# Down product of a sparse-expert layer on one core: three products of 224 columns into one PSUM place, three homes for the column parts, sums read straight from PSUM

## The reference

```python
def first_block(x, ...):
    ...                                   # gated mixing and dilated attention, w_out
    x = x + peer(rms_norm(x, norm2_g[layer]), w_query[layer], sub_keys[layer],
                 expert_u[layer], expert_v[layer])
    return rms_norm(x, final_norm_g)

def peer(xn, ...):                        # 8 heads pick 16 of 128 * 128 experts for each token
    ...
    act = jax.nn.gelu(jnp.einsum('td,thkd->thk', xb, u).astype(jnp.float32))
    return jnp.einsum('thk,thkd->td', (g * act).astype(xb.dtype), expert_v[e])

def second_block(x, ...):
    for layer in range(2):                # stick-breaking and indexed sparse attention, w_out, layer_norm
        h = hybrid_layer(h, w_in[layer], w_out[layer], ln_g[layer], ln_b[layer], rel_bias, topk)
    return h
```

## Time and profile before

| | |
|---|---|
| median of three runs (lowest to highest) | 1208.1 us (1206.0 to 1208.2) |
| time of the profiled execution | 1209.2 us |
| its span, first to last instruction | 1207.1 us |
| PE busy | 1179.2 us, 98% |
| weight loads busy | 1111.7 us, 92% |
| DVE, ACT, POOL busy | 759.0, 704.3, 741.8 us |
| granted TensorE clock over the span | 0.998 |
| stage "down" | from 547.1 to 882.2 us of the span |

### The profile page before, as it was taken

How to read it: one execution, slowest core, us unless ns; L and a number is a source line. 1 busy time by engine, 2 the same in 40 slices (tenths; PEclk the granted TensorE clock), 3 DMA queues, 4 the chain that set the end, 5 groups by cost and what they waited for, 6 DMA issues and landing times.

```text
span 1207.1 us, 24649 instructions
## 1 busy us (share of the span) xinstructions
PE 1179.2 (98%) x8981; PEld 1111.7 (92%) x8981; DVE 759.0 (63%) x1516; ACT 704.3 (58%) x1370; POOL 741.8 (61%) x349
## 2 busy tenths in 40 slices
PE   7999999999999999999999999999999999999997
PEld 6888999999999999999899999999999988899896
DVE  4454059995007778885777777777647746457446
ACT  5585445556558888775555555555564666456554
POOL 7747868888887777774232232331057776677674
PEclk9999999999999999999999999999999999999999
DMA  6735545665554444457778778777665434454443
GB/s 243 264 122 192 179 139 193 203 203 198 199 203 169 168 170 167 165 174 274 251 264 270 262 254 272 249 255 256 195 236 192 140 126 137 140 203 149 136 158 108
DMA packets 67145, 237.68 MB, mean 197 GB/s; under 512 B 8912, under 2 KB 10360, under 8 KB 66688
## 3 DMA queue, kind: packets, MB, share of 16 engines
q1 hardware_dynamic: 57024, 206.14, 50.9%
q0 software_dynamic: 7392, 25.68, 5.9%
q10 hardware_dynamic: 2656, 4.90, 1.1%
HBM read 232.30 MB, written 6.31 MB: 198 GB/s over the span
## 4 chain that ended last, share of the span: by engine, by line
PE 82%; DMA 5%; DVE 4%; ACT 4%; POOL 2%; issue 2%; DVEq 0%; SPq 0%; ACTq 0%
PE W L581 29%; PE W L825 6%; PE A L825 6%; PE A L625 5%; PE A L632 5%; PE A L627 5%; DMA ring<-exp_v 4%; PE A L827 3%; PE W L827 3%; PE A L605 2%; PE A L610 2%; PE A L606 2%; POOL ringl L490 2%; PE W L867 2%; ACT ringh L1316 1%
## 5 line engine op out<-in xcount | busy, mean ns | idle before, releaser
L490 POOL TENSOR_TENSOR ringl<-ring,ringh 128x1024 fp32r<-128x1024 f32 x137 | 341.6, 2514 | 132.4 <-ACT ringh L1120 112.9
L520 POOL TENSOR_TENSOR ringl<-ring,ringh 128x1024 fp32r<-128x1024 f32 x126 | 302.0, 2398 | 76.9 <-ACT ringh L1316 42.6
L581 PE MATMUL W<-XTh,ringh 128*128 128x256 f32 x1024 | 287.6, 281 | 0.1
L581 PE MATMUL W<-XTl,ringh 128*128 128x256 f32 x1024 | 282.8, 276 | 0.0
L581 PE MATMUL W<-XTh,ringl 128*128 128x256 f32 x1024 | 282.7, 276 | 0.0
L1316 ACT ACTIVATE ringh<-ring 128x1024 fp32r<-128x1024 f32 x181 | 190.5, 1053 | 34.9 <-DMA ring<-exp_v 32.6
L1120 ACT ACTIVATE ringh<-ring 128x1024 fp32r<-128x1024 f32 x135 | 141.7, 1058 | 116.3 <-PE A L632 47.2
L1769 DVE TENSOR_TENSOR ringl<-ring,ringh 128x1024 fp32r<-128x1024 f32 x127 | 155.4, 1224 | 69.2 <-ACT ringh L1316 61.3
L581 PEld LDWEIGHTS W<-XTh,ringh 128*128 128x128 f32 x1024 | 192.3, 188 | 0.3 <-ACTq L1227 0.3
L581 PEld LDWEIGHTS W<-XTl,ringh 128*128 128x128 f32 x1024 | 192.4, 188 | 0.0
L581 PEld LDWEIGHTS W<-XTh,ringl 128*128 128x128 f32 x1024 | 192.2, 188 | 0.0
(11 more groups left out here) (298 smaller groups left out, 2254.6 us busy)
## 6 DMA issues: line engine op xcount, KB each, us to landing
ring<-exp_u SPq DMA_DIRECT2D x128, 512.0 KB
ring<-exp_v SPq DMA_DIRECT2D x128, 512.0 KB
ring<-w SPq DMA_DIRECT2D x72, 512.0 KB
ring<-w_out SPq DMA_DIRECT2D x24, 512.0 KB
ring<-w_in SPq DMA_DIRECT2D x20, 512.0 KB
ring<-w_query SPq DMA_DIRECT2D x16, 512.0 KB
skewed<-scratch POOLq DMA_DIRECT2D x1, 2048.0 KB, 11.6
H<-lng POOLq DMA_DIRECT2D x2, 1024.0 KB, 6.5
```

What stands on the lines that cost most here:

```text
L490: pool.tensor_tensor(ringl[:, slot, :], ring[:, slot, :], ringh[:, slot, :].bitcast(F32), ALU.subtract)\
L520: pool.tensor_tensor(ringl[:, slot, :], ring[:, slot, :], ringh[:, slot, :].bitcast(F32), ALU.subtract)\
L581: last = pe.matmul(dst, stationary[a], moving[b], start=start and n == 0, stop=stop and n == 2, skip_group_check=True)
```

## The change

Down: a chunk is now `product` with 224 columns each time: high·high, high·low, low·high, all into columns 0 to 223 of the bank, and x and the gathered tokens go to columns 0 to 255 too. `HP` has three homes of 448 columns instead of two of 512 (`PARTS = 3`), so ACT and DVE prepare column n + 3 when PE has used column n. The last two columns are interleaved: the first two chunks of column 126, those of 127, the rest of 126, the rest of 127. At the end ACT makes `XTh` and DVE `XTl` straight from PSUM; `XTF`, needed for the way back only, is copied from PSUM afterwards, the first chunk of each pair by DVE, the second by ACT. PE waits for these copies before it writes into the bank again. At the end of each hybrid layer the second half of X of token block 0 is written after `add_half` and mean of block 1, instead of before.

```diff
-HP_END = 2 * TD + TS
+PARTS = 3
-        HP = sb("HP", [P, 2, 512], F32R)
+        HP = sb("HP", [P, PARTS, 2 * TD], F32R)
...
-            def down(slot, part, first=False, final=False):
-                for m in FIRST_CHUNKS if final else FIRST_COLUMN if first else range(KC):
+            def down_chunks(slot, part, chunks, first=False, final=False):
+                for m in chunks:
                     f = slice(m * P, (m + 1) * P)
...
-                    pe.matmul(DOWN[m][:, 0:2 * TD], ringh[:, slot, f], HP[:, part, 0:2 * TD], start=first, stop=False,
-                              skip_group_check=True)
-                    last = pe.matmul(DOWN[m][:, TD:2 * TD], ringl[:, slot, f], HP[:, part, TD:2 * TD], start=False, stop=final,
-                                     skip_group_check=True)
+                    last = product(DOWN[m][:, 0:TD], (ringh[:, slot, f], ringl[:, slot, f]),
+                                   (HP[:, part, TD:2 * TD], HP[:, part, 0:TD]), first, final)
...
+                elif n == NK - 2:
+                    down_chunks(slot, part, FIRST_CHUNKS[0:2])
+                    pe.wait_ge(lo_done, U_LAYER)
+                    pe.wait_ge(hl_done, NK)
+                    down_chunks((U_DOWN + NK - 1) % SLOTS, (NK - 1) % PARTS, FIRST_CHUNKS[0:2], final=True)
+                    down_chunks(slot, part, FIRST_CHUNKS[2:]).then_inc(unit_used, 1)
+                else:
+                    down_chunks(slot, part, FIRST_CHUNKS[2:], final=True).then_inc(unit_used, 1)
...
-                    column_high(6 * i + (n + 2), n % 2)
+                    column_high(6 * i + (n + PARTS), n % PARTS)
...
-            for p in range(KC // 2 + 1):
+            def keep_odd(p):
+                c = FIRST_CHUNKS[2 * p + 1]
+                act.wait_ge(tr_lo, 4 * 3 + p + 1)
+                act.activation(XTF[:, c, :], DOWN[c][:, 0:T], ACT.Copy).then_inc(xt_kept, 1)
+            for p in range(KC // 2):
...
                 for c in FIRST_CHUNKS[2 * p:2 * p + 2]:
-                    act.activation(XTF[:, c, 0:TD], DOWN[c][:, 0:TD], ACT.Copy).then_inc(xt_kept, 1)
+                    act.activation(XTh[:, c, :], DOWN[c][:, 0:T], ACT.Copy, scale=gain[:, 3, c:c + 1]).then_inc(tr_act, 1)
                 if p:
-                    for at in range(2 * p - 2, 2 * p):
...
+                    keep_odd(p - 1)
+            keep_odd(KC // 2 - 1)
...
-                if n + 2 < NK:
-                    column_low(n + 2, n % 2)
+                if n + PARTS < NK:
+                    column_low(n + PARTS, n % PARTS)
...
+            for p in range(KC // 2):
+                first_low(FIRST_CHUNKS[2 * p:2 * p + 2])
+                c = FIRST_CHUNKS[2 * p]
+                dve.tensor_copy(XTF[:, c, :], DOWN[c][:, 0:T]).then_inc(v_done, 1)
...
+                    if tb:
+                        finish(0, 1)
                     dve.wait_ge(mean_out, NB * layer + tb + 1)
...
-                    for half in range(2):
...
+                    finish(tb, 0)
+                finish(1, 1)
```

More of the change, by code:

```diff
@@ L824, in down @@
                         pe.wait_ge(col_done, AMID)
-                    pe.matmul(DOWN[m][:, 0:2 * TD], ringh[:, slot, f], HP[:, part, 0:2 * TD], start=first, stop=False,
-                              skip_group_check=True)
-                    last = pe.matmul(DOWN[m][:, TD:2 * TD], ringl[:, slot, f], HP[:, part, TD:2 * TD], start=False, stop=final,
-                                     skip_group_check=True)
+                    last = product(DOWN[m][:, 0:TD], (ringh[:, slot, f], ringl[:, slot, f]),
+                                   (HP[:, part, TD:2 * TD], HP[:, part, 0:TD]), first, final)
                     if final and m in FIRST_CHUNKS[1:-1:2]:
                         last.then_inc(pair_done, 1)
-                last.then_inc(unit_used, 1)
+                return last
+            def down(slot, part, first=False):
+                down_chunks(slot, part, FIRST_COLUMN if first else range(KC), first).then_inc(unit_used, 1)
             def ahead(i, s):
@@ L888, in _ @@
                     pe.wait_ge(hl_done, 6 * i + (n + 1))
-                    down((U_DOWN + n) % SLOTS, n % 2)
+                    down((U_DOWN + n) % SLOTS, n % PARTS)
             for n in range(6 * DOWN_TURNS + 2, NK):
@@ L892, in _ @@
                 pe.wait_ge(hl_done, n + 1)
-                down((U_DOWN + n) % SLOTS, n % 2, final=n == NK - 1)
+                slot, part = (U_DOWN + n) % SLOTS, n % PARTS
+                if n < NK - 2:
+                    down(slot, part)
+                elif n == NK - 2:
[6 more added lines that the diff above has]
+                    down_chunks(slot, part, FIRST_CHUNKS[2:], final=True).then_inc(unit_used, 1)
                 if n == TURN_AT:
@@ L904, in _ @@
                     for c in range(KC):
-                        pe.matmul(DOWN[c][:, 2 * TD:HP_END], ACC[:, c * P:(c + 1) * P], SEL, start=False, stop=False,
+                        pe.matmul(DOWN[c][:, TD:T], ACC[:, c * P:(c + 1) * P], SEL, start=False, stop=False,
                                   skip_group_check=True)
@@ L1331, in _ @@
                 if q == QUADS - 1:
-                    column_high(0, 0)
-                    column_high(1, 1)
+                    for col in range(PARTS):
+                        column_high(col, col)
                 j = amid_after(q)
@@ L1363, in _ @@
                 act.wait_ge(unit_used, U_DOWN + n + 1)
-                if n == TURN_AT:
-                    act.wait_ge(hl_done, -(-KC * T // TD))
-                    act.activation(XTF[:, :, TD:T], zeros[:, 0:TS].unsqueeze(1).broadcast_to([P, KC, TS]), ACT.Copy)
-                if n + 2 < NK:
-                    column_high(n + 2, n % 2)
+                if n + PARTS < NK:
+                    column_high(n + PARTS, n % PARTS)
                 next_high(U_DOWN + n + 1, 16 * (u // SLOTS + 1), u % SLOTS)
@@ L1796, in _ @@
             dve.nop().then_inc(h_final, NK - 1)
-            column_low(0, 0)
-            column_low(1, 1)
+            for col in range(PARTS):
+                column_low(col, col)
             finish_amid(AMID - 1)
@@ L1815, in first_low @@
                     dve.wait_ge(tr_act, high_seen[0] + at + 1)
-                    ins = dve.scalar_tensor_tensor(out=XTl[:, c, :], in0=XTF[:, c, :], scalar=gain[:, 3, c:c + 1],
+                    ins = dve.scalar_tensor_tensor(out=XTl[:, c, :], in0=DOWN[c][:, 0:T], scalar=gain[:, 3, c:c + 1],
                                                    in1=XTh[:, c, :].bitcast(F32), op0=ALU.mult, op1=ALU.subtract)
```

34 lines of the change are left out of this document (13 added, 21 removed).

## The result

The changed kernel takes 1224.9 us (median of four runs, 1223.7 to 1238.0), the kernel before, run beside it, 1208.15 us (median of four, 1206.0 to 1213.6). The medians lie 16.8 us apart, a ratio of 1.0139; the ratio of the means is 1.0156, with an interval of 1.008 to 1.0233, because the one run of 1238.0 us counts in it. Slower by 17 us, where 15.4 were forecast. For that one run there is a likely reason, taken up at the end: the stage up, which the change does not touch, takes some 14 us more in some executions.

The account below looks back on a forecast made before the run. The prediction took PE to bound the kernel (82% of the chain that ended last); +22.2 - 7 + 0 + 0.2 = +15.4 us gave a median of 1223.5 us, with the forecast covering 1220 to 1227 us (chance 0.50).

Parts of the forecast that it names:

- Part 1: Down's three equal matmuls: each lasts as long as its weight load, 335 ns a chunk instead of 313.3, +22.2 us.
- The load interval read from L905: Loads around L905, with 32-column matmuls, follow one another every 112 ns; taken as the load's own time.
- The step of 0.105 us after L827: Distance after down's 224-column matmul in the kernel before; lower bound of 315 ns a chunk, +1.8 us.
- The second rival: Down faster by streaming alone: a chunk costs 288 ns until DMA binds, 1198 us; chance 0.05.
- Part 2: Third home in down: PE's waits for the activations' low part shrink, -7 us, bounds 0 and -8.6.
- each wait gets shorter by 0.39 us, and where an addition lay in between by 1.28 more: Third home's saving on down's ten waits, four of them with an addition: 9.0 us, more than the 8.6 there.
- the other half of the part: Slower columns in down give the DMA 0.17 us more time each (2.680 against 2.507 us).
- The fifth rival: Third home leaves down's waits, since the DMA itself is late; only the product's cost remains: +22 us, 1230 us; chance 0.05.
- Part 3: End of down: 0.45 us gained before the layer's first matmul, given back at the transposes; 0, bounds -1 and +1.5 us.
- Part 4: End of a layer: DVE's moved half of X stands ahead of block 1's scaling; +0.2 us taken.

Follow-up runs that it names:

- E2: The kernel before with only L825 split into two 224-column matmuls, still two homes, two places and the old end: 1224.3 us, ratio 1.0128.
- E5: The changed kernel streaming only 128 of 224 columns in each of down's three matmuls: 1236.9 us (1229.0 to 1245.4).
- E7: The changed kernel streaming 192 of the 224 columns in each of down's three matmuls: 1224.3 us, ratio 1.0109.
- E1: The kernel before with three homes for the column parts and nothing else: 1208.1 us, ratio 0.9964.
- E8: The kernel before with only 3 of the 32 gathers of expert rows, the additions still running on old rows: 1203.1 us, ratio 0.9932.
- E10: The kernel before with three homes, interleaved last columns and the changed layer end, but the old 448 + 224 column chunks: 1221.3 us, ratio 1.0029.
- E6: The changed kernel streaming 256 instead of 224 columns in each of down's three matmuls, the 32 more being zeros: 1229.1 to 1256.4 us.

## Why the prediction was right, point by point

**Part 1** (+22.2 us) was right in mechanism and size. The load interval read from L905, 111.7 ns, is what down now shows, 335 ns a chunk. 3072 steps of 111.7 ns and 5.4 us for x and the gathered tokens are 348.5 us; the stage takes 348.6. E2 has it from that edit alone, E5 and E7 show that the stream is hidden behind the load. The step of 0.105 us after L827 was, as argued, no steady rate. The Trainium skill's rule for a load, its columns divided by 1.2 (page "TensorE: Matmul & The Clock Gate", section "LDWEIGHTS (loading the stationary operand)"), gives an estimate of 106.7 ns. That stays 5 ns under the 111.7 ns that down shows in every profile with three matmuls of 224 columns or fewer, as long as the clock is at 1.00, and the 5 ns are 15 us of this kernel. The second rival did not come true. The Trainium skill's formula that stood beside it (same page, section "Back-to-back issue gap") is there the gap of an isolated matmul, and the section says that in a stream of loads and matmuls both set the spacing; the prediction took it for such a stream. It gives an estimate of 95.8 ns; 111.7 were measured.

**Part 2** (-7 us) was right in the sum by the wrong cause. The waits inside down went, from 8.6 us to none, a little more than the term. The step that failed is "each wait gets shorter by 0.39 us, and where an addition lay in between by 1.28 more", and with it the whole share given to the third home. I took a wait to be the delay of its chain's end, and counted what leaves that chain. E1 removed just that and kept 8.1 of 8.6 us. The late DMA sets when PE goes on; a shorter chain behind it lets the engines catch up earlier and meet the next late DMA (ACT's waits for `exp_v` rose from 32.6 to 52.5 us). What removed the waits is the other half of the part, named and not priced: 0.17 us more a column, which is time for the transfers. E2 shows it with two homes, and E8 shows what made the transfers late. The fifth rival (the third home leaves the waits) was right in its mechanism and wrong in its time, because it left that out; without the slower column's slack 1230 would have been the figure. The sum came out near only because one unpriced effect replaced the one that was priced, and that is luck.

**Part 3** (0, bounds -1 and +1.5) was right also in its steps. The timeline of ACT at the end of down:

```profile
896.00 1.06 ACT L1330 ACTIVATE ringh<-ring 128x1024 fp32r<-128x1024 f32 x1 [2.29 <-PE W L581]
896.96 1.55 ACT L1396 ACTIVATE XTh<-A,gain 128x256 fp32r<-128x256 f32 x4
898.43 0.38 ACT L1388 ACTIVATE H<-A 128x256 f32<-128x256 f32 x1
```

and of PE:

```profile
897.64 0.28 PE L581 MATMUL W<-HP,ringl 128*128 128x224 f32 x1
899.03 0.36 PE L625 MATMUL A<-XTh,ringh 128*128 128x256 f32 x1 [1.11 <-ACT H L1388]
...
902.30 1.94 PE L979 MATMUL W<-cst,H 128*128 128x128 f32 x16 [0.21 <-ACT H L1388]
```

With E = 897.92 the first matmul starts at E + 1.11 (forecast 1.0), released by ACT's copy of the first pair (L1388), the transposes at E + 4.38 (forecast 4.4, before 4.35). What is won at the first place (0.34 us) is lost at the second.

**Part 4** (+0.2, for two layers) was too high by a little. In the last layer the reciprocal of block 1 comes 2.94 us after the end of the last matmul, before 2.89 us: +0.05, since `add_half` now starts as soon as PE is done. The other layer was not measured by itself, and is taken to be alike.

```profile
1216.43 0.69 DVE L1994 SCALAR_TENSOR_TENSOR X<-X,A 128x512 f32<-128x512 f32 x1 [0.47 <-PE A L758]
...
1218.02 1.28 DVE L2018 SCALAR_TENSOR_TENSOR H<-X,stat,H 128x1024 f32<-128x1024 f32 x1
1219.33 0.16 DVE L2022 RECIPROCAL stat<-stat 128x1 f32<-128x1 f32 x1
```

The sum of the parts by the traces is +22.2 - 8.6 + 0 + 0.1 = +13.7 us. The other 2.6 of the 16.3 us between the two spans lie before down (2.2) and in the layers (0.4), where the profiles of all runs differ by as much. That forecast and the measured difference of medians lie 1.4 us apart is closer than the reasons deserve.

## What to carry to other kernels

Where each matmul brings new weights, compare its load with its stream. Up to 224 columns a step of this kernel cost its load, 111.7 ns; at 256 columns it cost 113.3 or 117.7. Read the load interval where matmuls are tiny, and do not cut a long matmul whose length hides a load. A wait behind a late DMA is not shortened by shortening the chain behind the DMA: ask first whether the transfers keep pace, by slowing the consumer or taking other traffic away. A term can be right through two errors, so try its cause alone.

## What the hardware showed beside that

Steps of 256 columns (float32r, new weights each time) come at one of two distances, and keep it for long stretches. Busy times in the up product, 180 to 360 us, of the changed kernel and of E10, which have the same code there:

```profile
180.00:360.00 180.00, 180.00 (x1591) 180.00 (x1590) 107.64 (x364) 94.71 (x202) 159.15 (x67) 1.00 0.58 199
```

```profile
180.00:360.00 180.00, 180.00 (x1531) 180.00 (x1530) 103.87 (x364) 91.29 (x194) 153.47 (x64) 1.00 0.57 192
```

1591 against 1531 matmuls at the same clock, with loads without a pause in both, 113.3 and 117.7 ns a step. Over the 3072 steps of up that is 13.5 us, and down starts at 562.3 us in E10 and 562.0 in E7 instead of 547 to 549. In E6 up ran at the shorter distance and down at the longer. The layers change between the two within one execution, in the kernel before as well: there 118 steps in a row from 915 us are 118 ns apart, and 133 in a row from 1097 us are 113. So both distances occur in both kernels. That a longer up is also what made the unprofiled runs of 1221 to 1227 us of the kernel before, and that of 1238.0 of the changed one, is likely from their size, and not shown. What decides between the two distances was not tried. A comparison of kernels like these by their medians mixes the two, as in E10; one stage by stage shows where each was at work.
